# Hybrid decoder layer on one core: products added in pairs in PSUM, the seventh product of a block issued behind the first of the next, three down blocks in seven products, and raw x for the first tile

## The chip, the cores and the metric

The kernel runs on one core of a Trainium2 chip. The metric is the device time of one execution in microseconds (us), as the median of several; lower is better. TensorE (PE) does the matrix products, VectorE (DVE), ScalarE (ACT) and GpSimd (POOL) read and write SBUF, and DVE and ACT also read PSUM, where matrix products end. SyncE (SP) issues most transfers.

## What is computed

```python
def decoder_layer(x, ...):
    h, new_hist, v = hybrid_mixer(rms_norm(x, mix_pre_g), conv_hist, ...)
    x = x + rms_norm(h, mix_post_g)
    f = swiglu(rms_norm(x, ffn_pre_g), w_gate, w_up, w_down)
    return x + rms_norm(f, ffn_post_g), new_hist, v

def hybrid_mixer(xn, ...):
    z = xn @ w_in                                   # 1024 -> 7 x 1024
    u, v, b_gate, c_gate, x_in, r_a, r_b = jnp.split(z, SPLITS, axis=-1)
    u = gelu(u)
    v = layer_norm(gelu(v), sgu_ln_g, sgu_ln_b)
    y_a = (u * chunk_spatial_mix(v, w_s, b_s)) @ w_a_out
    c_in = c_gate * x_in
    y_b = (b_gate * short_conv([conv_hist, c_in], conv_w)) @ w_b_out
    return (sigmoid(r_a) * y_a + sigmoid(r_b) * y_b) @ w_o, ..., v

def swiglu(x, w_gate, w_up, w_down):                # 1024 -> 2816 -> 1024
    return (silu(x @ w_gate) * (x @ w_up)) @ w_down
```

There are 1024 prompt tokens and 8 samples of one token each, all in float32. `rms_norm` multiplies a row by its gain and by the root of its inverse mean square, so the root can also be multiplied in behind a product with a weight.

## The kernel before

**Numbers.** A float32 operand is kept as a high and a low part (`hi`, `lo`, type fp32r), and a product of two operands is three matmuls: hi by hi, hi by lo, lo by hi (`three`).

**Blocks and runs.** Activations lie transposed, channels on partitions, tokens along the free side (two groups of 516, each in two halves of 258 columns with the samples). The weights come in blocks of 256 columns: `B_U` 0, `B_C` 4 (here C, X and B blocks take turns), `B_RA` 16, `B_RB` 20, `B_A` 24 (w_a_out), `B_B` 28 (w_b_out), `B_F` 32 (gate and up blocks in turn), `B_D` 54 to 65 (w_down in three slices of K of `MP` = 4 blocks each, whose sums are added in `g`). `RUNS` lists them; the last blocks are run in two halves (`R_LAST`, `R_LAST + 1`, with 258 columns in their operations). v and w_o are computed in another form, with 512 columns, at the start and in the middle.

**Seven products.** Most blocks are done as Strassen-Winograd, seven products P0 to P6 in place of eight, each of `kps(b)` x 6 matmuls of 258 columns (24 at kps 4, and 18 in the first slice of K, where kps is 3). The operands of the token side are sums and differences of quarters, kept in eight slots of `tp`. The weight side is prepared per run: DVE adds the quarters (`sums`, into `ring_f`), ACT makes the high parts (`prepare`, L1240), POOL the low parts (`ring_lo`, L1095), and PE waits for POOL by `w_lo`. Blocks in `QORDER` are plain: four halves of 48 x kps / 4 matmuls.

**PSUM.** There are four pairs of banks, X, Y, Z and W. `PBANK` says in which pair each product ends. ACT copies P0 (`s1`, L1251), DVE forms from there and from the pairs the four quarters of the result: `c11`, `u1`, `u3`, `u2`, `c22`, `c12`, `c21`, seven operations a run. A product into a pair waits until the pair was read.

**The engines' queues.** Each engine works through one list written out by hand. ACT's has, beside `s1` and `prepare`, the activation functions of the quarters, and where a new stage begins the high parts of its operands: `a_split`, `bt_split`, and `t_split` (L1583) for the three slices of w_down, the wheels here called wheel 0, 1 and 2. DVE's has the low parts `a_rest`, `t_rest` (L2385), and for w_down the additions into `g` (L2484). The operands of the down wheels are written to DRAM as hidden rows are ready and read back by DMA into `tp_f`.

**Start.** The tiles of v are taken in the order samples, then the eight tiles of 128 tokens. Rows are normalised (`x_norm`), turned by PE, split, and multiplied with `wv_hi_t` and `wv_lo_t`, the parts of w_v, whose eight rows of 128 channels come one by one.

## Time and profile before

| | |
|---|---|
| median of 3 runs | 1603.2 us (1603.16 to 1603.54) |
| span of the profiled execution, first to last instruction | 1601.0 us |
| time of a run outside the span (1603.2 - 1601.0) | 2.2 us |
| PE busy | 1590.6 us, 99% |
| DVE, ACT, POOL busy | 1081.9, 559.8, 703.9 us |
| granted TensorE clock, mean | 0.999 of full speed |
| PE's share of the chain that ended last | 95% |

The profile gives for each engine how long it was busy, why it waited and for whom. Since PE is busy for almost the whole span, what counts is the number of matmuls, the time of one, and every moment in which PE waits for a semaphore of another engine. L12 is line 12 of the kernel before.

### The profile page before, as it was taken

The numbers are of one execution on the slowest core, as the hardware profiler recorded it, in microseconds if no ns is written. First come the engines' busy times: TensorE is split into PE (matmuls) and PEld (weight loads), VectorE is DVE, ScalarE is ACT, GpSimd is POOL, SyncE is SP. The second block draws the span as 40 slices with busy tenths as digits, with TensorE's granted clock in tenths as the row PEclk, the third lists the DMA queues.
The fourth block names the chain that finished last, engine by engine and source line by source line (L and its number), as shares of the span: only waits on it lengthen the run. The fifth ranks groups of instructions, "written<-read, shape, count | busy, mean of one in ns | idle before, by whom it ended". The sixth has DMA issues, their size and how long they took to land.

```text
span 1601.0 us, 30253 instructions
## 1 busy us (share of the span) xinstructions
PE 1590.6 (99%) x12427; PEld 1542.2 (96%) x12427; DVE 1081.9 (68%) x1463; ACT 559.8 (35%) x852; POOL 703.9 (44%) x512
## 2 busy tenths in 40 slices
PE   9999999999999999999999999999999999999998
PEld 6889999999999999999978999999999999999997
DVE  8757857797793338868965666766666666575766
ACT  4222332222223336333434532333332233352544
POOL 1011534544544444644730324544444443545375
PEclk9999999999999999999999999999999999999999
DMA  6202011431423333474423313533333345472723
GB/s 216 79 1 80 27 54 34 126 96 44 126 82 110 109 106 121 149 242 133 148 91 120 131 41 110 155 105 100 106 104 104 105 124 178 153 239 80 238 107 133
DMA packets 155283, 184.38 MB, mean 115 GB/s; under 512 B 7355, under 2 KB 138035, under 8 KB 155147
## 3 DMA queue, kind: packets, MB, share of 16 engines
q1 hardware_dynamic: 154987, 182.41, 35.7%
q8 instruction: 99, 1.62, 0.4%
q14 instruction: 37, 0.30, 0.1%
q10 hardware_dynamic: 160, 0.04, 0.0%
HBM read 133.74 MB, written 48.72 MB: 114 GB/s over the span
## 4 chain that ended last, share of the span: by engine, by line
PE 95%; DVE 1%; DMA 1%; POOL 1%; issue 1%; SPq 0%; ACT 0%; DVEq 0%; ACTq 0%; POOLq 0%
PE ps L414 91%; PE ps L449 1%; PE ps L526 1%; DMA pre_gain<-in_mix_pre_g 1%; DVE tp L2213 1%; PE ps L669 0%; PE ps L653 0%; PE ps L424 0%; DMA tp_f<-hid_dram 0%; SPq L783 0%; DVE s_bc L2232 0%; POOL ring_lo L1108 0%; POOL ring_lo L1095 0%; PE ps L503 0%; DVE g L2234 0%
## 5 line engine op out<-in xcount | busy, mean ns | idle before, releaser
L414 PE MATMUL ps<-tp,ring_hi 128*128 128x258 f32 x7292 | 1182.9, 283 | 0.5 <-issue 0.3
L414 PEld LDWEIGHTS ps<-tp,ring_hi 128*128 128x128 f32 x7292 | 1010.6, 190 | 0.9 <-issue 0.5
L414 PE MATMUL ps<-tp,ring_lo 128*128 128x258 f32 x3646 | 744.8, 283 | 0.0
L414 PEld LDWEIGHTS ps<-tp,ring_lo 128*128 128x128 f32 x3646 | 571.3, 190 | 0.0
L1095 POOL TENSOR_TENSOR ring_lo<-ring_f,ring_hi 128x512 fp32r<-128x512 f32 (+1 forms) x228 | 328.3, 1460 | 365.1 <-DVE ring_f L1840 212.5
L1095 POOL TENSOR_TENSOR ring_lo<-stage,ring_hi 128x512 fp32r<-128x512 f32 (+1 forms) x199 | 304.7, 1540 | 400.3 <-ACT ring_hi L1240 399.6
L1240 ACT ACTIVATE ring_hi<-ring_f 128x512 fp32r<-128x512 f32 (+1 forms) x228 | 142.6, 627 | 519.9 <-DVE ring_f L1835 196.2
L1240 ACT ACTIVATE ring_hi<-stage 128x512 fp32r<-128x512 f32 (+1 forms) x199 | 122.0, 617 | 121.1 <-PE ps L414 63.5
L1832 DVE TENSOR_TENSOR ring_f<-stage 128x512 f32<-128x512 f32 (+1 forms) x57 | 46.8, 821 | 135.2 <-PE ps L414 82.7
L1853 DVE TENSOR_TENSOR s_a<-ps,s_a 128x516 f32<-128x516 f32 (+1 forms) x58 | 39.8, 686 | 51.9 <-PE ps L414 51.4
L414 PE MATMUL ps<-tp 128*128 128x512 f32 (+1 forms) x384 | 72.0, 340 | 0.0
L414 PEld LDWEIGHTS ps<-tp 128*128 128x128 f32 x384 | 59.0, 189 | 8.2
L2385 DVE TENSOR_TENSOR tp<-tp_f,tp 128x2064 fp32r<-128x2064 f32 (+1 forms) x24 | 56.2, 2343 | 13.7 <-ACT tp L1583 13.7
L1251 ACT ACTIVATE s_a<-ps 128x516 f32<-128x516 f32 (+1 forms) x58 | 34.2, 590 | 77.3 <-PE ps L414 60.2
L1864 DVE TENSOR_TENSOR s_a<-ps,s_a 128x516 f32<-128x516 f32 (+1 forms) x58 | 39.6, 683 | 30.5 <-PE ps L414 30.4
L1583 ACT ACTIVATE tp<-tp_f 128x2064 fp32r<-128x2064 f32 (+1 forms) x24 | 42.8, 1784 | 39.8 <-DMA tp_f<-hid_dram 33.2
L414 PE MATMUL ps<-wv_hi_t,tp 128*128 128x512 f32 x192 | 54.1, 397 | 0.0
L2420 DVE TENSOR_TENSOR hq<-hq,q 128x516 f32<-128x516 f32 x40 | 47.0, 1176 | 1.1
L1835 DVE TENSOR_TENSOR ring_f<-ring_f,stage 128x512 f32<-128x512 f32 (+1 forms) x57 | 42.8, 751 | 2.2 <-PE ps L414 2.2
L414 PEld LDWEIGHTS ps<-wv_hi_t,tp 128*128 128x128 f32 x192 | 35.7, 188 | 8.0
L1837 DVE TENSOR_TENSOR ring_f<-stage 128x512 f32<-128x512 f32 (+1 forms) x57 | 39.6, 695 | 0.0
L1847 DVE TENSOR_TENSOR s_bc<-ps,s_a 128x516 f32<-128x516 f32 (+1 forms) x21 | 14.0, 668 | 36.8 <-PE ps L414 36.6
(243 smaller groups left out, 1453.9 us busy)
## 6 DMA issues: line engine op xcount, KB each, us to landing
stage<-in_w_in SPq DMA_DIRECT2D x24, 1024.0 KB, 5.9
ht_dram<-ht SPq DMA_DIRECT2D x44, 258.0 KB, 4.2
hid_dram<-hq SPq DMA_DIRECT2D x40, 258.0 KB, 3.1
stage<-in_w_gate SPq DMA_DIRECT2D x10, 1024.0 KB, 6.6
stage<-in_w_up SPq DMA_DIRECT2D x10, 1024.0 KB, 5.3
tp_f<-hid_dram SPq DMA_DIRECT2D x16, 516.0 KB, 5.5
tp_f<-ht_dram SPq DMA_DIRECT2D x16, 516.0 KB, 8.7
stage<-in_w_down SPq DMA_DIRECT2D x8, 1024.0 KB, 7.1
```

Source lines behind the costliest of these rows:

```text
L414: ins = pe.matmul(o, w, xc, start=first and n == 0, stop=last and n == 2)
L1095: pool.tensor_tensor(lo, src, hi.bitcast(f32), SUB).then_inc(w_lo, 1)
L1240: act.activation(w_ring(b, p, kp)[0], src, ACT.Copy).then_inc(w_hi, 1)
L1251: act.activation(s_a[:, gs], reg(Z, gs), ACT.Copy).then_inc(s1_done, 1)
L1583: act.activation(slot(s, 0, both, ks), slot_f(s, 1, both, ks), ACT.Copy).then_inc(t_hi, 1)
L1832: ins = dve.tensor_tensor(out, a21, a22, ADD)
L1835: ins = dve.tensor_tensor(out, ring(ring_f, b, 1, kp), a11, SUB)
L1837: ins = dve.tensor_tensor(out, a11, a21, SUB)
L1853: dve.tensor_tensor(s_a[:, gs], reg(X, gs), s_a[:, gs], ADD).then_inc(u1_done, 1)
L1864: dve.tensor_tensor(s_a[:, gs], reg(Z, gs), s_a[:, gs], ADD).then_inc(u2_done, 1)
L2385: dve.tensor_tensor(slot(s, 1, both, ks), slot_f(s, 1, both, ks), slot_v(s, 0, both, ks), SUB).then_inc(t_lo, 1)
L2420: dve.tensor_tensor(hq[:, n], hq[:, n], q[:, n], MUL).then_inc(hid_ready, 1)
```

## The change

Four parts, in the words of the code:

1. **Wheel.** The first block of each slice of w_down (`B_D`, `B_D + 4`, `B_D + 8`) leaves `QORDER` and runs in seven products. Seven operands a slice stand in place of eight, in slots that turn from slice to slice (`SLOTS_D`), so that product p finds its operand in a slot that an earlier product of the run before has left.
2. **Pairs in PSUM.** P2 is accumulated onto P0 in Y, and P6 onto P4 in X. c11 is then Y as it stands, read by the user itself; `c11` and `u1` are gone as operations of DVE. P2 must wait until ACT has copied P0 (`s1_done`), P6 until `c22` has read P4.
3. **Seventh product behind.** For runs without plain neighbours, P0 of run r + 1 is issued ahead of P6 of run r (`piped`).
4. **v's start.** The samples and the first tile of 128 tokens are multiplied with x times gain, without the root, which comes in as the scale of the gelu. The samples' high and low parts stand in one operand of 40 rows, so that their three matmuls a step become two. The 43 warming transposes of `ident` become 16.

```diff
-PBANK = [Z, W, Y, X, Z, Y, X]
+PBANK = [Y, W, Y, Z, X, Z, X]
...
+D_WHEEL = [5] + SLOTS_B
+SLOTS_D = [[D_WHEEL[(p - n) % 8] for p in range(7)] for n in range(3)]
...
-QORDER.update({b: FIRST_HALF_EVEN for b in (B_D, B_D + MP, B_D + 2 * MP)})
...
+def piped(run):
+    return 2 < run < len(RUNS) - 1 and RUNS[run][0] not in QORDER and RUNS[run + 1][0] not in QORDER
...
+V_STEPS = "S0 H0 s0 S1 H1 L0 s1 S2 H2 L1 s2 S3 H3 L2 S4 H4 s3 L3 N0 S5 H5 s4 S6 H6 s6 s5 H7 s7 S7 " \
+          "L4 L5 L6 N1 L7 l0 l1 l2 l3 l4 l5 N2 l6 l7".split()
...
+            def turn_raw():
+                pe.wait_ge(x_in[0], 16)
+                pe.wait_ge(gain_in, 16)
+                for k in range(KT):
+                    pe.transpose(ps[:, 6, NS * k:NS * k + NS], x_rows[0][0:NS, 128 * k:128 * k + 128], ident[0:NS, 0:NS])
...
             pe.wait_ge(consts, 4)
-            turn_ident(32)
-            turn_norm(0)
-            turn_ident(11)
-            v_sample_tile()
-            v_first_tile(1)
+            turn_ident(8)
+            turn_raw()
+            v_start()
             v_first_tile(2)
...
+            def product(r, p):
+                if p == 6 and piped(r):
+                    issue(r + 1, 0)
+                if p or not piped(r - 1):
+                    issue(r, p)
+
+            def issue(r, p):
...
+                if p == 2:
+                    pe.wait_ge(s1_done, SIDX[r])
+                elif p == 5:
+                    pe.wait_ge(u2_done, SIDX[r])
+                elif p == 6:
+                    pe.wait_ge(c22_done, SIDX[r])
+                elif RUNS[r - 1][0] != b:
+                    bank_free(r - 1, PBANK[p])
...
+            def t_begin(n, r, nb):
+                s1(r)
+                prepare(nb, 0, 2)
+                if n == 1:
+                    c11_down(r)
+                t_split(n, 1)
+                prepare(nb, 2, 3)
+                t_split(n, 2)
...
+                dve.wait_ge(u4_done, SIDX[r])
+                dve.tensor_tensor(c_22, c_22, s_c[:, gs], ADD).then_inc(d_part, 1)
+                dve.tensor_tensor(c_12, c_12, s_c[:, gs], ADD).then_inc(d_part, 1)
+                dve.tensor_tensor(c_21, c_21, s_turn[r % 2][:, gs], ADD).then_inc(d_part, 1)
+                dve.wait_ge(prod_done, done(r, 4))
+                dve.wait_ge(d_part, parts + 1)
+                dve.tensor_tensor(c_22, reg(X, gs), c_22, ADD).then_inc(c22_done, 1)
```

PE's list in the FFN, from P4 of one run to P4 of the next: each row is the first matmul of a product, and in brackets what it waits for. Before:

```order
L414 MATMUL ps<-tp,ring_hi 128x258 [waits s1_done,w_lo]
...
L414 MATMUL ps<-tp,ring_hi 128x258 [waits c11_done,w_lo]
...
L414 MATMUL ps<-tp,ring_hi 128x258 [waits u1_done,w_lo]
...
L414 MATMUL ps<-tp,ring_hi 128x258 [waits u2_done,w_lo]
...
L414 MATMUL ps<-tp,ring_hi 128x258 [waits c22_done,w_lo]
...
L414 MATMUL ps<-tp,ring_hi 128x258 [waits c12_done,w_lo]
...
L414 MATMUL ps<-tp,ring_hi 128x258 [waits c21_done,w_lo]
...
L414 MATMUL ps<-tp,ring_hi 128x258 [waits s1_done,w_lo]
```

In the changed kernel, from P2 of an up block's run (r) to P2 of the next run; the fifth row is P0 of run r + 1, which waits until c11 of run r was read (`hid_ready`), the sixth P6 of run r:

```order
L442 MATMUL ps<-tp,ring_hi 128x258 [waits s1_done,w_lo]
...
L442 MATMUL ps<-tp,ring_hi 128x258 [waits c12_done,w_lo]
...
L442 MATMUL ps<-tp,ring_hi 128x258 [waits c21_done,w_lo]
...
L442 MATMUL ps<-tp,ring_hi 128x258 [waits u2_done,w_lo]
...
L442 MATMUL ps<-tp,ring_hi 128x258 [waits hid_ready,w_lo]
...
L442 MATMUL ps<-tp,ring_hi 128x258 [waits c22_done,w_lo]
...
L442 MATMUL ps<-tp,ring_hi 128x258 [waits u4_done,w_lo]
...
L442 MATMUL ps<-tp,ring_hi 128x258 [waits s1_done,w_lo]
```

The wait for `s1_done` moved from P4 to P2, so that only P6 of the run before and P1 stand between the product that is copied and the one that waits for the copy; P6 waited for `u1_done` and now waits for `c22_done`.

ACT's list where the second slice of w_down begins (wheel 1), around the copy of P0 of the old slice's last block (L1251) and the operands of the new slice (L1583). Before:

```order
L1583 ACTIVATE tp<-tp_f_55 128x8x258 [waits t_in1]
L1251 ACTIVATE s_a<-ps 128x516 [waits c21_done,prod_done]
L1583 ACTIVATE tp<-tp_f_54 128x8x258 [waits t_in0]
L1240 ACTIVATE ring_hi<-stage_71 128x512 [waits prod_done,stage_in0]
L1583 ACTIVATE tp<-tp_f_56 128x8x258 [waits t_in2]
L1240 ACTIVATE ring_hi<-stage_71 128x512 [waits prod_done,stage_in0]
L1583 ACTIVATE tp<-tp_f_50 128x8x258 [waits total_in0]
```

Changed (L1361 is `s1`, L1722 `t_split`, L1414 the new copy of c11, L1331 `prepare`):

```order
L1722 ACTIVATE tp<-tp_f_53 128x8x258 [waits t_in0]
L1361 ACTIVATE s_bc<-ps 128x516 [waits c21_done,prod_done]
...
L1414 ACTIVATE g<-ps 128x516 [waits prod_done]
L1722 ACTIVATE tp<-tp_f_55 128x8x258 [waits total_in0]
L1331 ACTIVATE ring_hi<-stage_71 128x512 [waits prod_done,stage_in0]
L1722 ACTIVATE tp<-tp_f_54 128x8x258 [waits t_in2]
...
L1722 ACTIVATE tp<-tp_f_56 128x8x258 [waits total_in2]
L1331 ACTIVATE ring_hi<-stage_71 128x512 [waits prod_done,stage_in0]
L1361 ACTIVATE s_a<-ps 128x516 [waits c21_done,prod_done]
```

The first operand still stands ahead of `s1` of the last block of the old slice, but P2 of that block waits for this `s1` now, and four operands stand ahead of the copy of P0 of the new slice's first block (the last row), which had no such copy.

DVE's list in a run of the second slice, from the first operation behind c11 to the start of c12. Before (L1853 is u1, L1858 u3, L1864 u2, L1869 c22, L2484 the addition of c22 into `g`, L1835 and L1837 are sums of weights):

```order
L1853 TENSOR_TENSOR s_a<-ps,s_a 128x516 [waits c11_done,prod_done]
L1858 TENSOR_TENSOR s_bc<-ps,s_a 128x516 [waits u1_done]
L1835 TENSOR_TENSOR ring_f<-ring_f,stage_72 128x512 [waits s_sum,stage_in1,prod_done]
L1864 TENSOR_TENSOR s_a<-ps,s_a 128x516 [waits u3_done,prod_done]
L1869 TENSOR_TENSOR s_bc<-ps,s_a 128x516 [waits u2_done,d_tmp]
L1837 TENSOR_TENSOR ring_f<-stage_72 128x512 [waits stage_in1,prod_done]
L2484 TENSOR_TENSOR g<-g,s_bc 128x516 [waits c22_done]
L1875 TENSOR_TENSOR s_bc<-ps,s_bc 128x516 [waits prod_done,u3_done]
```

Changed (L2031 is u2, L2036 u4, L2644 to L2646 the additions of parts, L2649 the new c22):

```order
L2031 TENSOR_TENSOR s_bc<-ps,s_bc 128x516 [waits s1_done,prod_done]
L2036 TENSOR_TENSOR s_bc<-ps,s_bc 128x516 [waits u2_done]
L2019 TENSOR_TENSOR ring_f<-ring_f,stage_71 128x512 [waits s_sum,stage_in0,prod_done]
L2644 TENSOR_TENSOR g<-g,s_bc 128x516 [waits u4_done]
L2645 TENSOR_TENSOR g<-g,s_bc 128x516
L2646 TENSOR_TENSOR g<-g,s_bc 128x516
L2649 TENSOR_TENSOR g<-ps,g 128x516 [waits d_part,prod_done]
L2021 TENSOR_TENSOR ring_f<-stage_71 128x512 [waits stage_in0,prod_done]
```

u1 is gone, and three additions of parts into `g` moved ahead of c22, for which P6 waits.

## Rows read from the trace of the kernel before

**Rows 1.** the page: engines, matmuls of L414 with mean ns of one

```profile
PE 1590.6 (99%) x12427; PEld 1542.2 (96%) x12427; DVE 1081.9 (68%) x1463; ACT 559.8 (35%) x852; POOL 703.9 (44%) x512
...
L414 PE MATMUL ps<-tp,ring_hi 128*128 128x258 f32 x7292 | 1182.9, 283 | 0.5 <-issue 0.3
```

**Rows 2.** PE's waits over the whole span: waited for, us in total, times, longest

```profile
PE ps L509 <- POOL ident L1073: 1.8, 1, 1.8
...
PE ps L414 <- POOL ring_lo L1108: 0.3, 1, 0.3
PE ps L414 <- issue: 0.3, 1, 0.3
PE ps L414 <- POOL ring_lo L1095: 0.3, 1, 0.3
```

**Rows 3.** windows: length, busy us and count for each engine, PEclk, DMA share, GB/s

```profile
200.00:220.24 20.24, 20.24 (x171) 20.24 (x170) 10.90 (x23) 6.04 (x10) 6.47 (x6) 1.00 0.17 53
1410.00:1430.00 20.00, 19.45 (x160) 19.07 (x159) 16.21 (x12) 12.41 (x11) 15.03 (x6) 1.00 1.09 350
```

**Rows 4.** chain that ended last, a piece of the start: start, us, what

```profile
29.67 11.12 PE ps L449 x48
```

**Rows 5.** timeline of PE at the start: start us, us, engine line op

```profile
9.35 0.69 PE L449 MATMUL ps<-wv_hi_t,smp_hi 128*8 128x512 f32 x2
...
34.16 0.62 PE L449 MATMUL ps<-wv_hi_t,tp 128*128 128x512 f32 x2
```

**Rows 6.** timeline of ACT at the start, first row of w_v

```profile
5.31 1.06 ACT L1214 ACTIVATE wv_hi_t<-gv 128x1024 fp32r<-128x1024 f32 x1 [1.39 <-DMA gv<-in_w_in]
```

**Rows 7.** windows of the first 9.35 us, two of them, columns as above

```profile
1.76:4.00 2.24, 2.24 (x11) 2.24 (x12) 0.06 (x1) 1.68 (x4) 0.00 (x0) 1.00 0.73 159
...
7.50:9.35 1.85, 1.85 (x22) 1.75 (x20) 1.08 (x3) 1.51 (x4) 0.25 (x2) 1.00 1.04 425
```

**Rows 8.** timeline of DVE in an FFN pair: c21 of a run

```profile
1129.18 0.69 DVE L1880 TENSOR_TENSOR q<-ps,s_a 128x516 f32<-128x516 f32 x1 [1.53 <-PE ps L414]
```

**Rows 9.** timeline of ACT in the same pair: the silu behind c21

```profile
1129.91 0.64 ACT L1575 ACTIVATE q<-q 128x516 f32<-128x516 f32 x1
```

**Rows 10.** timeline of ACT at the last gate block and the first of w_a_out

```profile
607.69 0.63 ACT L1240 ACTIVATE ring_hi<-stage 128x512 fp32r<-128x512 f32 x1 [0.40 <-PE ps L414]
...
610.90 0.58 ACT L1251 ACTIVATE s_a<-ps 128x516 f32<-128x516 f32 x1
```

**Rows 11.** timeline of DVE at the same place

```profile
620.81 3.45 DVE L2100 TENSOR_TENSOR tp_f<-gv,tp_f 128x1024 f32<-128x1024 f32 x2
624.18 1.26 DVE L2102 TENSOR_TENSOR tp_f<-mix_s,tp_f 128x16 f32<-128x16 f32 x1
```

**Rows 12.** timeline of ACT at the second w_b_out block

```profile
741.57 0.58 ACT L1251 ACTIVATE s_a<-ps 128x516 f32<-128x516 f32 x1
```

**Rows 13.** timeline of DVE at wheel 0

```profile
1359.32 1.76 DVE L2385 TENSOR_TENSOR tp<-tp_f,tp 128x1548 fp32r<-128x1548 f32 x1
```

**Rows 14.** timeline of ACT at wheel 1

```profile
1399.57 0.53 ACT L1240 ACTIVATE ring_hi<-stage 128x384 fp32r<-128x384 f32 x1 [0.43 <-PE ps L414]
1400.00 1.92 ACT L1583 ACTIVATE tp<-tp_f 128x2064 fp32r<-128x2064 f32 x1
1401.82 0.57 ACT L1251 ACTIVATE s_a<-ps 128x516 f32<-128x516 f32 x1
```

**Rows 15.** timeline of DVE at wheel 2

```profile
1496.42 3.10 DVE L2385 TENSOR_TENSOR tp<-tp_f,tp 128x2064 fp32r<-128x2064 f32 x1
1499.44 1.79 DVE L2484 TENSOR_TENSOR g<-g,s_bc 128x516 f32<-128x516 f32 x1
```

**Rows 16.** timeline of DVE at the tail: c21 of R_LAST

```profile
1573.30 0.43 DVE L1880 TENSOR_TENSOR s_bc<-ps,s_a 128x258 f32<-128x258 f32 x1 [0.51 <-PE ps L414]
```

**Rows 17.** timeline of ACT at the tail: table load, last s1

```profile
1575.43 1.28 ACT L1692 ACT_TABLE_LOAD   x1
...
1576.83 0.37 ACT L1251 ACTIVATE s_a<-ps 128x258 f32<-128x258 f32 x1
```

More of the change, by code:

```diff
@@ L409, in _, with three @@
         def _(pe):
-            def three(outs, w_h, w_l, x_h, x_l, first, last):
+            def three(outs, w_h, w_l, x_h, x_l, first, last, onto=False):
                 ins = None
@@ L413, in three @@
                     for o, xc in zip(outs, x):
-                        ins = pe.matmul(o, w, xc, start=first and n == 0, stop=last and n == 2)
+                        ins = pe.matmul(o, w, xc, start=first and n == 0, stop=last and n == 2, skip_group_check=onto)
                 return ins
```

795 lines of the change are left out of this document (450 added, 345 removed).

## The prediction

> **What bounds the kernel now.** I read the page first: PE is busy for 99% of the span, while DVE has 68%, ACT 35% and POOL 44% [rows 1]. The reader should see that the kernel is bound by the number of matmuls and by nothing else on average. The waits of PE come second: one of 1.8 us at the very start, which the change leaves as it is, and three of 0.3 us [rows 2]. So a stall inside can be taken away for less than 1 us, and anything more must come from fewer matmuls. The windows give the time of one: in a steady stretch 168 matmuls (one run of seven products, 24 each) take 20.24 us, 0.1205 us each (the count there has a few over, since a matmul's own duration overlaps the next) [rows 3]. A product is 2.89 us at kps 4, 2.17 us at kps 3, and 1.45 us in the two half runs. A matmul lasts 283 ns by its own row [rows 1], so the end of a product is seen 0.16 us after the next may start. With 512 columns 48 matmuls take 11.12 us, 0.232 us each [rows 4].
>
> **What the change removes.**
> - Down blocks. A plain block has 48 x kps matmuls, one of seven products 42 x kps. Three blocks with kps 3, 4 and 4 lose 6 x 11 = 66 matmuls: 66 x 0.1205 = **-7.95 us**.
> - Start. PE multiplies from 9.35 and reaches the second tile's low-high products at 34.16 [rows 5]. In the changed list the samples need 32 matmuls of 512 columns in place of 48. The first weight row has its high part from 5.31 us on [rows 6]; raw x of the first tile is turned by about 6.6, multiplied by the gain by 7.9 and split by 9.0, by ACT and DVE operations as long as those of the list before (1.06 us at ACT). The samples' first matmul can start at about 7.75, and from there 80 matmuls (samples 32, first tile 48) x 0.232 = 18.6 us and three turns of about 0.9 us are worked off with about 0.9 us of waits: 29.95. That is **-4.2 us** against 34.16. Bounds: -4.5 if nothing waits, -2.5 if the clock takes part (below).
> - The stalls at 812 and 1417 to 1421: the places are relieved (seven operands a slice, two DVE operations fewer a run). **-0.85 us** [rows 2], bounds 0 and -0.9.
>
> Together -13.0 us.
>
> **What it adds: shorter leashes.** PE must now find three things ready in each run: the copy of P0 (`s1`) before P2, u2 before P5, c22 before P6. I laid the lists of the changed kernel over the durations of the trace.
> - Steady runs, no stall. Let T be the end of P6. c21 takes 0.69 [rows 8], the silu behind it 0.64 [rows 9], `s1` 0.58 [rows 10]: done at T + 2.0. P2 starts at T + 2.73 (P1's 2.89 less 0.16). That leaves 0.7 us, and a prepared block (0.63 at ACT) fits in but no more. Some 50 runs look like this. Cost 0; if the cover were gone it would be paid 50 times, so it is the first thing to look at afterwards.
> - From the r_b blocks to w_a_out. P6 of the run before the last ends at 610.5 (607.6, where ACT's next weight row waits for PE [rows 10], plus the P0 put before it). c21, a gate and `a_split` of about 2.1 us stand ahead of `s1`, which ran from 610.90 to 611.5 before; it ends at 614.4 now where P2 could start at 613.2: 1.2 us. Then P6 and the plain halves of w_a_out, which follow at once, wait for c22 and c12, and these stand behind `a_rest` and the totals, 3.45 + 1.26 us where POOL works too [rows 11]. I get 1.9 us at least and 5.2 at most in sum, and take **+3.0**, above the lower end because the trace shows DVE's list full there.
> - w_b_out. `s1` of its second block ran from 741.57 to 742.15 behind an operand [rows 12], and P2 would start at about 741.0; P6 of the run before w_b_out waits 0.25 us. **+1.2** (0.4 to 2.2).
> - Wheel 0. u2 of the last FFN run stands behind `t_rest` (1.76 us each at kps 3 [rows 13]) and the totals of the hidden rows. **+1.0** (0 to 3).
> - Wheel 1. An operand of 1.92 us stands between a weight row and `s1`: the three ran from 1399.57 to 1402.39 [rows 14], T + 2.9, and P2 starts at T + 2.0, since P1 is of kps 3 here: +0.9. The next `s1` stands behind four operands and the last weight row, whose sum is made behind c12: +0.8 (0 to 2). **+1.7**. The operands land fast enough, with the DMA at 350 GB/s [rows 3].
> - Wheel 2. The same with kps 4: +0.36 for the first; the second `s1` waits for a sum behind c12, three additions into `g` (0.69 to 1.79 each) and two `t_rest` of 2.9 and 3.1 us [rows 15]: +1.5 (0.5 to 3.2). **+1.9**.
> - Tail. In `R_LAST` the copy stands behind c21, a square and a gain, T + 2.35 where P2 could start at T + 1.29 (P1 is 1.45 long): +1.05. In `R_LAST + 1` a table load stands there too: from c21 at 1573.30 [rows 16] to the end of `s1` at 1577.20 [rows 17] it took 3.9 us, of which 0.75 (the addition now made by c21 itself) goes, 3.15 against 1.29: +1.85. P6 behind the root of y: +0.3 (0 to 0.7). **+3.2**, bounds 2.0 and 3.7.
>
> DVE's u2 and c22 in steady runs come 2 us ahead of their need (T + 9.4 against T + 11.6), because two operations of 0.69 are gone.
>
> **The sum.** -13.0 + 3.0 + 1.2 + 1.0 + 1.7 + 1.9 + 3.2 = -13.0 + 12.0 = **-1.0 us**. Against the profiled execution: 1601.0 to 1600.0. The median is 2.2 us above that span, and nothing in the change touches what lies around it: 1603.2 - 1.0 = **1602.2 us**. At the lower bounds of the stalls (1.9, 0.4, 0, 0.9, 0.86, 2.0: 6.1) it is 1596.3; at the upper bounds (5.2, 2.2, 3, 2.9, 3.6, 3.7: 20.6) 1610.8.
>
> **A rule that speaks against the change.** DVE's additions of two inputs in SBUF take 1.79 us instead of 0.69, and a 16-column one 1.26 us, where GpSimd works at the same time [rows 15, 11]. The Trainium skill, "SBUF — State Buffer", section "Who interferes with whom", calls the port pair of DVE and GpSimd an exclusive lock that is held for a whole instruction, and the trace agrees as far as that 16-column operation waits about 1.1 us, no more than a GpSimd operation lasts. By that rule the three additions of parts that moved ahead of c22 could wait for GpSimd up to three times, 1.1 us each; that would be the upper bound at wheels 1 and 2, and is a way into the slower rival.
>
> **The rivals.**
> - *Stalls at their lower bounds.* DVE loses two operations of 0.69 us a run; its lists at the wheels may be so much earlier that only ACT's order costs. For it speaks that PE shows almost no stall now, though the lists are as full. Against it: at the tail and at wheel 1 the lateness is ACT's own, and 2.9 us are left whatever DVE does. Time about 1596.5 (1594 to 1599).
> - *Slower: ACT's queue at wheels 1 and 2.* `s1` of the new slice's first block stands behind a weight row whose sum DVE makes behind c12. c12 can't come before P5, and if DVE's additions run at 1.8 us in place of 0.69, three of them and two `t_rest` delay the sum by about 4 us. Each microsecond in which the sum ends later than 0.85 us before P6's end is a microsecond for PE. That is 3 us more at each of two wheels: 1602.2 + 6 = 1608. For it: the 1.79 and 3.10 us rows. Against it: the seven operands arrive over a whole run, and the additions may fall between GpSimd's.
> - *The clock at the start.* The windows say that the granted clock was 1.00 from the first, which is 2.4 GHz, yet 11 transposes took 2.24 us (0.20 each) in the first window, and 22 took 1.85 us (0.084 each) just before the samples [rows 7]. PE had then worked without a pause. With 16 warming transposes in place of 43, and waits for x between them, the first matmuls of v may still go at the slow pace: at about double the time, 7 or 8 pairs lose some 0.23 us a matmul, up to 3 us. The time would be about 1605. The Trainium skill, "TensorE: Matmul & The Clock Gate", Part 1, says that throttled is the default and activity releases it; the pace of the transposes agrees and the row of the granted clock doesn't. I count it 1 in 10, because PE is busy for some 5 of the 6 us before.
> - *The change doesn't save its matmuls* is excluded: the order of PE's list holds 66 and 16 fewer.
>
> **How the numbers follow.** 0.2% is 3.2 us, about what a measurement of this kernel can tell from no change. The forecast (stalls eat nearly all, 1598.5 to 1606) gets 0.47, of which 0.12 lie under 1600, 0.32 within and 0.03 above; the first rival 0.28, nearly all faster; the slower one 0.15; the clock 0.10, half within and half above. Together faster 0.38, same 0.39, slower 0.23. The range 1595.5 to 1609 leaves out the last of either side.
>
> **What would show it.** Right: the second tile's matmuls near 30 us; PE stalls of 1 to 3 us at about 610 to 630, 740, wheels 1 and 2 and in the last 30 us, released by ACT's `s1` or DVE's c22; none in the FFN. Wrong: PE waits in every FFN run (then 50 times any of it), `s1` never named among PE's releasers (then the time is that of the first rival), or matmuls at half pace before 12 us. Accumulating onto a bank that ACT has just read is shown by no row here. The 258-column matmuls of one product already accumulate without a gap, so I take 0 for it; a cost of only 0.2 us a run, some 50 times, would put the time above my range.

## The result and the profile after

The changed kernel took 1625.7 us (median of 4 runs, 1624.9 to 1627.5), the kernel before 1603.4 (4 runs, 1603.2 to 1603.6): a ratio of 1.0139, 95% interval 1.0125 to 1.0154. It is slower by 22.4 us. Forecast were 1602.2 us and a range of 1595.5 to 1609, with a chance of 0.23 for slower, so the prediction was wrong, and outside its range. The profiled execution has a span of 1624.6 us; L12 is now line 12 of the changed kernel.

The page, engines and the product's own matmuls (answers to [rows 1]):

```profile
PE 1589.9 (98%) x12335; PEld 1540.6 (95%) x12335; DVE 1001.5 (62%) x1376; ACT 558.1 (34%) x867; POOL 722.7 (44%) x524
...
L442 PE MATMUL ps<-tp,ring_hi 128*128 128x258 f32 x7248 | 1182.3, 285 | 23.1 <-ACT s_bc L1361 5.2
```

PE is as busy as before (1590.6 us there) with 92 records of matmuls fewer (66 are saved in the down blocks and 16 in the samples; the rest are transposes at the start), and the line of the products has 23.1 us of idle time ahead of it where it had 0.5. So two things happened: PE waits, and a part of its matmuls lasts longer. PE's waits (answers to [rows 2], without the two at the very start and end that both kernels have) say for whom:

```profile
PE ps L442 <- ACT s_bc L1361: 5.2, 5, 1.5
PE ps L442 <- DVE g L2649: 4.7, 3, 2.2
PE ps L442 <- ACT s_a L1361: 4.2, 3, 1.8
PE ps L442 <- DVE s_a L2042: 3.5, 1, 3.5
PE ps L442 <- DVE s_a L2031: 3.3, 1, 3.3
PE ps L442 <- DVE q L2042: 2.2, 1, 2.2
PE ps L488 <- ACT raw_hi L1366: 1.9, 1, 1.9
...
PE ps L442 <- POOL ring_lo L1199: 0.2, 1, 0.2
```

The changed code waits in 14 places inside (all the L442 rows with ACT or DVE as releaser), in sum 23.1 us. ACT's copy of P0 (L1361, `s1`) has 9.4 us of it, DVE's c22 (L2042, in the wheels L2649) 10.4, u2 (L2031) 3.3. None of them lies in the FFN between 1000 and 1300 us. The windows (columns as in [rows 3]) show where matmuls last longer:

```profile
10.43:14.40 3.97, 3.97 (x10) 2.33 (x11) 3.90 (x6) 3.97 (x6) 1.10 (x1) 0.57 1.03 412
200.00:220.24 20.24, 20.24 (x171) 20.24 (x170) 10.15 (x23) 6.89 (x12) 5.88 (x6) 1.00 0.16 53
627.00:633.00 6.00, 5.38 (x32) 5.41 (x33) 4.16 (x7) 3.14 (x4) 0.61 (x1) 0.72 0.00 0
1374.00:1384.00 10.00, 6.74 (x36) 6.57 (x35) 8.83 (x11) 3.00 (x6) 3.42 (x4) 0.66 0.50 160
1540.00:1544.00 4.00, 3.74 (x19) 3.77 (x20) 1.92 (x4) 3.25 (x6) 1.94 (x2) 0.57 0.02 4
```

In a steady stretch the product is what it was: 20.24 us with 171 records, like the first of [rows 3]. Around four places the granted clock is lowered, and around 717 us as well (0.59 from 716.7 to 720.8); the mean over the span (0.993) hides it. Inside each stretch it is 0.50 for 3.4 us, that is 1.2 GHz, and PE had stood idle just before: 1.94 us at the start, 2.25, 3.50, 3.26 and 2.21 us inside. Wheel 0 has two such stretches in a row, so inside there are five. A 258-column matmul takes 0.215 us there instead of 0.1205 (E5 shows the rows), so 16 are done in 3.4 us, which would take 1.9: a stretch costs 1.5 us where PE is busy through all of it. Wheel 0's two lasted from 1376.24 to 1383.07 by the record of the clock, and PE stood idle until 1377.46, so together they cost 2.5; the one in wheel 2, from 1540.08, cost 1.4. The five inside cost 6.9 us.

**The account.** Fixed points of the program say where the time came from: the transposes of `hist_rows` come at 105.41 us (106.6 before, -1.2), the first product of w_o comes at 806.88 (795.5, +11.4), eight products of `ones` and `q` in the tail at 1601.91 (1578.84, +23.1). A stall costs 0.24 us more than the idle time that the view shows, here called its trail: 0.16 because a matmul's shown end trails the next possible start, and 0.08 because the second matmul behind a stall starts late as well (0.195 us after the first, in E5 too). By terms: matmuls saved -7.95, start -1.2, 14 stalls +23.1, their trails +3.4, five stretches +6.9, the stalls of before with their trails -1.6, one new wait for `ring_lo` +0.5: +23.1 against +23.6 between the spans. 0.5 us is open.

What lies behind the stalls is seen in the engines' lists. DVE at the first w_a_out blocks (answers to [rows 11]; L2254 is `a_rest`, L2042 c22):

```profile
617.69 2.35 DVE L2254 TENSOR_TENSOR tp<-gv,tp 128x1024 fp32r<-128x1024 f32 x2
619.97 0.17 DVE L2256 TENSOR_TENSOR tp<-mix_s,tp 128x16 fp32r<-128x16 f32 x1
...
622.26 3.46 DVE L2254 TENSOR_TENSOR tp<-gv,tp 128x1024 fp32r<-128x1024 f32 x2 [0.79 <-ACT tp L1475]
625.64 1.23 DVE L2256 TENSOR_TENSOR tp<-mix_s,tp 128x16 fp32r<-128x16 f32 x1
626.79 0.68 DVE L2042 TENSOR_TENSOR q<-ps,q 128x516 f32<-128x516 f32 x1
```

PE has been idle since 625.4, ready for P6. c22 comes at 626.79 because `a_rest` stands ahead of it, and its last two rows take 3.46 and 1.23 us where the same two took 2.35 and 0.17 just before; GpSimd's next low parts run from 622.82 to 626.84.

At w_b_out the delay begins in SP's queue (L973 loads of gate rows, L956 the first operands of w_b_out):

```profile
685.77 16.04 SPq L973 DMA_DIRECT2D q<-ra_dram  x4
...
702.88 5.88 SPq L956 DMA_DIRECT2D tp_f<-ob_dram  x3
```

The loads of `ob_dram` were issued at 702.88, behind four gate loads whose issues stretch over 16.04 us from 685.77; before, they were issued at 696.50. That is 6.4 us later, of which 4.0 is what the whole program had lost by then; the rest goes with the gate loads, the last of which may start only when the last quarter of a run is gated, and this quarter comes from P6, behind P0 (2.89 us) of the next run. In E4, where P6 stands in its own place, `ob_dram` is issued at 696.32, and PE is as far on there as in the kernel before. ACT's `b_split` starts at 711.74 (704.23 before), and on DVE its low part stands ahead of c22:

```profile
713.70 2.31 DVE L2317 TENSOR_TENSOR tp<-tp_f,tp 128x2064 fp32r<-128x2064 f32 x1 [4.76 <-ACT tp L1529]
715.93 0.69 DVE L2042 TENSOR_TENSOR s_a<-ps,s_bc 128x516 f32<-128x516 f32 x1
```

DVE in wheel 1, up to c22 (L2649; L2545 is `t_rest`, L2644 to L2646 the additions of parts; answers to [rows 15]):

```profile
1448.05 3.41 DVE L2545 TENSOR_TENSOR tp<-tp_f,tp 128x2064 fp32r<-128x2064 f32 x1
1451.38 1.77 DVE L2644 TENSOR_TENSOR g<-g,s_bc 128x516 f32<-128x516 f32 x1
1453.08 0.68 DVE L2645 TENSOR_TENSOR g<-g,s_bc 128x516 f32<-128x516 f32 x1
...
1454.29 0.68 DVE L2649 TENSOR_TENSOR g<-ps,g 128x516 f32<-128x516 f32 x1
```

The operation on the operand and the first addition are drawn out (3.41 and 1.77 us) while GpSimd works, until 1452.60; the next takes 0.68. What this drawing out alone costs PE no run shows, since none moves GpSimd's work there. PE waits 2.18 us, until 1455.12. In wheel 0 two `t_rest`, a sum of weights and totals of the hidden rows stand ahead of u2, the last of them the first row here:

```profile
1374.94 1.76 DVE L2545 TENSOR_TENSOR tp<-tp_f,tp 128x1548 fp32r<-128x1548 f32 x1
1376.63 0.69 DVE L2031 TENSOR_TENSOR s_a<-ps,s_a 128x516 f32<-128x516 f32 x1
```

At the start PE took the slow turns up to 7.77 and then waited (answers to [rows 5, 7]):

```profile
6.48 1.53 PE L528 MATMUL ps<-ident,x_rows 128*128 128x128 f32 x8
...
10.43 0.85 PE L488 MATMUL ps<-wv_hi_t,raw_hi 128*128 128x512 f32 x2 [1.94 <-ACT raw_hi L1366]
...
32.86 0.97 PE L477 MATMUL ps<-wv_hi_t,tp 128*128 128x512 f32 x3 [0.19 <-ACT tp L1312]
```

### The profile page after: what moved, and what is told of

The parts are those of the page before. It is cut to its first block, busy times and chain, and to the rows that moved or that the text cites. A ratio compares the mean times of both kernels' runs of the same rounds, so it can differ in the third digit from the quotient of the medians.

```text
span 1624.6 us, 30012 instructions
## 1 busy us (share of the span) xinstructions
PE 1589.9 (98%) x12335; PEld 1540.6 (95%) x12335; DVE 1001.5 (62%) x1376; ACT 558.1 (34%) x867; POOL 722.7 (44%) x524
## 4 chain that ended last, share of the span: by engine, by line
PE 88%; DVE 6%; issue 2%; ACT 2%; DMA 1%; POOL 0%; DVEq 0%; SPq 0%; ACTq 0%; POOLq 0%
PE ps L442 83%; DVE tp L2545 2%; PE ps L488 1%; PE ps L587 1%; PE ps L477 1%; DMA tp_f<-ob_dram 1%; PE ps L454 0%; PE ps L759 0%; ACT tp L1722 0%; PE ps L743 0%; DVE tp L2375 0%; DVE g L2644 0%; DVE ring_f L2019 0%; ACT tp L1474 0%; PE ps L572 0%
## 5 line engine op out<-in xcount | busy, mean ns | idle before, releaser
L442 PE MATMUL ps<-tp,ring_hi 128*128 128x258 f32 x7248 | 1182.3, 285 | 23.1 <-ACT s_bc L1361 5.2
L442 PEld LDWEIGHTS ps<-tp,ring_hi 128*128 128x128 f32 x7248 | 1009.7, 191 | 25.8 <-issue 17.3
L442 PE MATMUL ps<-tp,ring_lo 128*128 128x258 f32 x3624 | 743.0, 284 | 0.0
L442 PEld LDWEIGHTS ps<-tp,ring_lo 128*128 128x128 f32 x3624 | 570.5, 191 | 0.0
L1186 POOL TENSOR_TENSOR ring_lo<-ring_f,ring_hi 128x512 fp32r<-128x512 f32 (+1 forms) x240 | 348.9, 1475 | 356.1 <-DVE ring_f L2024 209.7
L1186 POOL TENSOR_TENSOR ring_lo<-stage,ring_hi 128x512 fp32r<-128x512 f32 (+1 forms) x196 | 293.0, 1504 | 415.7 <-ACT ring_hi L1331 415.1
L1331 ACT ACTIVATE ring_hi<-ring_f 128x512 fp32r<-128x512 f32 (+1 forms) x240 | 150.0, 625 | 535.7 <-DVE ring_f L2019 182.2
L1331 ACT ACTIVATE ring_hi<-stage 128x512 fp32r<-128x512 f32 (+1 forms) x196 | 120.7, 619 | 253.6 <-PE ps L442 185.3
L2016 DVE TENSOR_TENSOR ring_f<-stage 128x512 f32<-128x512 f32 (+1 forms) x60 | 58.2, 970 | 104.1 <-DMA stage<-in_w_in 53.9
L442 PE MATMUL ps<-tp 128*128 128x512 f32 (+1 forms) x384 | 72.1, 340 | 0.0
L442 PEld LDWEIGHTS ps<-tp 128*128 128x128 f32 x384 | 59.0, 189 | 8.2
L2053 DVE TENSOR_TENSOR q<-ps,s_a 128x516 f32<-128x516 f32 x17 | 11.8, 696 | 72.2 <-PE ps L442 72.2
L442 PE MATMUL ps<-wv_hi_t,tp 128*128 128x512 f32 x192 | 54.1, 397 | 0.0
L2021 DVE TENSOR_TENSOR ring_f<-stage 128x512 f32<-128x512 f32 (+1 forms) x60 | 51.8, 864 | 0.0
L2545 DVE TENSOR_TENSOR tp<-tp_f,tp 128x2064 fp32r<-128x2064 f32 (+1 forms) x21 | 51.1, 2435 | 0.0
L2031 DVE TENSOR_TENSOR s_bc<-ps,s_bc 128x516 f32<-128x516 f32 (+1 forms) x31 | 21.2, 685 | 47.0 <-PE ps L442 47.0
L2031 DVE TENSOR_TENSOR s_a<-ps,s_a 128x516 f32<-128x516 f32 (+1 forms) x30 | 20.5, 685 | 42.5 <-PE ps L442 42.3
L442 PEld LDWEIGHTS ps<-wv_hi_t,tp 128*128 128x128 f32 x192 | 35.6, 188 | 8.0
L2024 DVE TENSOR_TENSOR ring_f<-stage,ring_f 128x512 f32<-128x512 f32 (+1 forms) x60 | 40.3, 671 | 0.0
L1722 ACT ACTIVATE tp<-tp_f 128x2064 fp32r<-128x2064 f32 (+1 forms) x21 | 37.4, 1781 | 5.5 <-DMA tp_f<-hid_dram 3.7
L1186 POOL TENSOR_TENSOR tp<-tp_f,tp 128x512 fp32r<-128x512 f32 x4 | 5.7, 1464 | 61.5 <-ACT tp L1331 61.5
```

Of the source, the lines that this page charges most:

```text
L442: ins = pe.matmul(o, w, xc, start=first and n == 0, stop=last and n == 2, skip_group_check=onto)
L1186: pool.tensor_tensor(lo, src, hi.bitcast(f32), SUB).then_inc(w_lo, 1)
L1331: act.activation(w_ring(b, p, kp)[0], src, ACT.Copy).then_inc(w_hi, 1)
L1722: act.activation(slot(s, 0, both, ks), slot_f(s, 1, both, ks), ACT.Copy).then_inc(t_hi, 1)
L2016: ins = dve.tensor_tensor(out, a21, a22, ADD)
L2021: ins = dve.tensor_tensor(out, a11, a21, SUB)
```

## The experiments

Each ran beside the kernel before on the same chip; ratios are to that kernel. E1 to E4 ran together, E5 to E8, E9 and E10.

### E1: `s1` put ahead of the operands

```diff
-                if last:
-                    a_split(1)
                 s1(r)
                 if last:
+                    a_split(1)
                     a_split(0)
...
             prepare(B_B + 1, 4, 6)
+            s1(B_B + 1)
             bt_split(3)
             prepare(B_B + 1, 6)
-            s1(B_B + 1)
...
+                s1(r + 1)
                 t_split(n, 4)
                 prepare(nb, 6)
...
-            for e in range(12, 16):
+            for e in range(12, 15):
                 sq_gain(e)
-            act.activation(warm, eps, ACT.Sqrt)
             s1(R_LAST + 1)
+            sq_gain(15)
+            act.activation(warm, eps, ACT.Sqrt)
```

> The changed kernel with ScalarE's copy of P0 (s1) put ahead of what stands before it in ACT's list at the six places where PE waited for it: ahead of a_split(1), bt_split(3), t_split(1,0), t_split(1,4), t_split(2,0), t_split(2,4), and at the tail ahead of the last square and gain and of the table load. Theory A (s1 is late because of what is queued before it on ACT, 9.4 us of stalls in all, and nothing else is late at these places): these seven waits go, 1625.7 - 9.4 = about 1616.5. Rival B (the runs behind them are late for DVE as well, so that the stall moves to the next c22): under half is given back, 1621 or more. The stalls on c22 and u2 (about 10.4 and 3.3 us) and four of the five stretches at the halved clock stay.

Measured: 1623.1 us (1620.7 to 1624.0), 1.0117 [1.0102, 1.0132]. PE's waits in it:

```profile
PE ps L442 <- DVE g L2652: 6.9, 4, 3.2
PE ps L442 <- DVE s_a L2034: 4.1, 3, 3.3
PE ps L442 <- DVE q L2045: 3.6, 1, 3.6
PE ps L442 <- DVE s_a L2045: 3.2, 1, 3.2
...
PE ps L442 <- ACT s_bc L1361: 0.2, 1, 0.2
```

ACT's copies had 9.4 us and have 0.2. The waits for c22 and u2 had 13.7 us and have 18.1, and seven stretches at half clock stand inside where there were five (+2.6 us). So 9.2 us and their trails taken away shortened the span by 2.8: half only moved to the next wait, which was late on its own account, and the longer waits cost more clock. That is rival B. The copy alone is not the cause of the loss.

### E2: c22 put ahead of the operands

```diff
+                c22(r, q[:, 3], q[:, 1])
                 if last:
                     a_rest(2)
-                c22(r, q[:, 3], q[:, 1])
...
+                if last:
+                    b_rest(1)
...
                 dve.tensor_tensor(c_22, reg(X, gs), c_22, ADD).then_inc(c22_done, 1)
+                sums(nb, 1)
+                if n is not None:
+                    t_rest(n, 1)
...
+                dve.tensor_tensor(c_12, c_12, s_c[:, gs], ADD).then_inc(d_part, 1)
+                dve.tensor_tensor(c_21, c_21, s_turn[r % 2][:, gs], ADD).then_inc(d_part, 1)
...
+                    t_rest(0, 5)
+                    u2(r + 2)
                 hidden_total(j, 2, hq)
                 hidden_total(j, 1, hq)
```

> The changed kernel with DVE's list reordered: c22 ahead of a_rest(2), ahead of b_rest(1), and in the down runs ahead of a weight sum and of two of the three additions into g; at wheel 0 t_rest(0,5) and u2 ahead of the last three hidden totals. Theory A (DVE's own order makes P6 and P5 wait, and each such stall of over 2 us also costs 1.7 us at the halved clock): 2.2 + 3.5 + 2.2 + 2.2 of c22 go, the 3.3 of u2 falls to about 1, and with them about 8 us of halved clock: 1625.7 - 12.4 - 8 = about 1605. Rival B (the clock's loss has nothing to do with these stalls): 1613. Rival C (DVE is simply full there, so that the wait moves on to the next read): over 1616.

Measured: 1624.7 us (1624.2 to 1626.0), 1.0130 [1.0115, 1.0145].

```profile
PE ps L442 <- ACT s_bc L1361: 9.0, 6, 2.8
PE ps L442 <- ACT s_a L1361: 5.2, 3, 1.9
PE ps L442 <- DVE s_bc L2048: 2.9, 1, 2.9
PE ps L442 <- DVE q L2048: 2.3, 1, 2.3
```

c22 is gone from the waits at both boundaries and in the last two wheels, wheel 0's stall for u2 fell from 3.3 to 0.8 us, and still the waits inside sum to 23.1 us again: 2.9 and 2.3 for c12 (L2048) at the boundaries, where the plain halves of w_a_out and w_b_out need its bank first, 14.2 for ACT's copies in place of 9.4, one of them 2.8, 1.6 for c22 at 1380.9 in the first slice, where it was not waited for before, and 1.1 at 480 us for a weight block that landed late. Three stretches at half clock stand inside, where there were five. Neither list alone carries the loss; behind the delay in one stands one of the same size in the other. The time is that of rival C, the wait moved on, though not to DVE's reads alone.

### E3: work for PE in the gap of the start

```diff
                         if k == 7:
                             ins.then_inc(v_full, 1)
+                        if n == 0:
+                            turn_ident(16)
```

> The changed kernel with 16 transposes of ident put between the first matmuls of the samples and the first of the raw tile, where PE was idle for 1.9 us before a stretch at half clock. Theory A (the halved clock behind the idle stretch is what makes the start late): the wait remains, the halved stretch goes, 1.7 us less: 1624.0. Rival B (the clock falls whatever PE does there, or the transposes run slowly and push the first matmul back): same or up to 1 us slower.

Measured: 1625.8 us (1624.3 to 1628.2), 1.0137 [1.0122, 1.0153].

```profile
10.43:14.40 3.97, 3.97 (x24) 2.67 (x22) 3.94 (x6) 3.97 (x5) 0.72 (x1) 1.00 1.02 414
```

```profile
23.34 0.64 PE L488 MATMUL ps<-wv_lo_t,smp_v 128*8 128x512 f32 x2 [0.65 <-POOL wv_lo_t L1167]
...
32.83 2.36 PE L477 MATMUL ps<-wv_hi_t,tp 128*128 128x512 f32 x9 [0.19 <-ACT tp L1314]
```

With transposes in the gap the clock stays at 1.00 (0.57 in the changed kernel). That alone doesn't show that the idle time lowered it: in E1, E2, E4 and E7 the start is as in the changed kernel, PE is idle there for 1.55 to 1.67 us, and the clock stays at 1.00 too. What it cost is shown by all five: the second tile comes at 32.80 to 32.83 us, as behind the lowered clock (32.86), and PE waits 0.65 to 0.97 us at 23.3 us for GpSimd's low parts of w_v, of which it makes two in 9.6 us. The time didn't move. At the start the lowered clock lay within the wait for GpSimd, and cost nothing.

### E4: P6 back in its own place

```diff
-    return 2 < run < len(RUNS) - 1 and RUNS[run][0] not in QORDER and RUNS[run + 1][0] not in QORDER
+    return False
```

> The changed kernel with the seventh product in its old place: P6 of a run is issued before P0 of the next. All else stays. Theory A (piping is what makes the copy of P0 late, since P6 ends one product later, c21 and what ACT makes of it come later, and only P1 stands between): the seven waits for s1, 9.4 us, go, while P6 has one product less of cover for c22: 4 of the c22 stalls grow by up to 2.9 us each, less what SP's queue gains in front of w_b_out: between 1616 and 1628, and the FFN stays without stalls. Rival B (the piping is what covers c22 in every run): a stall in each of some 50 runs, 0.5 us or more each, 1650 or more.

Measured: 1625.6 us (1624.5 to 1627.4), 1.0133 [1.0116, 1.0150]. In PE's waits c22 in the wheels has this row:

```profile
PE ps L442 <- DVE g L2649: 11.6, 7, 3.8
```

Of ACT's copies only two are waited for, 1.5 and 0.4 us, since two products, P0 and P1, stand between P6 of the run before and P2, and not one. c22 is waited for 16.5 us with its other rows, where it was 10.4, since P6 comes a product earlier, and seven stretches at half clock stand inside. Taken out alone, the third part of the change is neither gain nor loss here, to within about 4 us.

### E5: a ladder of stalls in the kernel before

To price a stall and find from which length the clock falls, additions into a scratch row of DVE stand ahead of u1 in seven FFN runs of the kernel before, 7 to 13 of them. Their results aren't used.

```diff
+                for _ in range({3: 7, 4: 8, 5: 9, 6: 10, 7: 11, 8: 12, 9: 13}.get(j, 0)):
+                    link(dve.tensor_tensor(s_c[:, :], s_a[:, :], s_a[:, :], ADD))
                 u1(r)
```

> The kernel before, with DVE's u1 made late in seven FFN gate runs, 40 us apart, by 7, 8, 9, 10, 11, 12 and 13 extra additions of 128x516 (some 0.75 us each) ahead of it; their result is not used. PE then has stalls that differ by about 0.75 us from rung to rung, from about 0.5 to about 5 us, in a stage that has none. Theory A (a stall has two prices, its own length, and above some length between 1.5 and 2.3 us a further 1.7 us in which the matmuls go at the halved clock): the rungs above it show a stretch with a granted clock of 0.5 behind the stall and lose 1.7 us, those above about 3 us lose up to 3.4; those below show none. Rival B (the halved clock in the changed kernel has another cause): no stretch at a lower clock on any rung.

Measured: one run of 1620.5 us, span 1618.8, 17.8 longer than the span before. It has no second execution, so its price per stall rests on this one trace. The two shortest gave no stall, the others 0.44, 1.17, 1.89, 2.63 and 3.36 us (ending at 1126.9, 1168.9, 1211.5, 1256.3 and 1301.8). The windows behind three of them:

```profile
1168.00:1173.00 5.00, 4.16 (x34) 4.19 (x35) 4.93 (x8) 1.58 (x3) 1.29 (x1) 1.00 0.00 0
1211.00:1216.00 5.00, 4.52 (x25) 4.55 (x26) 4.77 (x8) 1.91 (x4) 1.30 (x2) 0.66 0.01 3
1301.00:1308.00 7.00, 6.16 (x31) 6.20 (x31) 6.04 (x9) 3.27 (x6) 2.66 (x3) 0.54 0.00 1
```

The stall of 1.17 us left the clock at 1.00; those of 1.89 and 2.63 us (1256 to 1260: 0.57) went with one stretch at 0.50, the one of 3.36 with two, the first of which began 1.2 us before PE went on. Behind the third, on PE's timeline:

```profile
1212.57 1.06 PE L414 MATMUL ps<-tp,ring_hi 128*128 128x258 f32 x4
...
1213.86 1.06 PE L414 MATMUL ps<-tp,ring_hi 128*128 128x258 f32 x4
```

Six matmuls stand between the starts of two groups, in 1.29 us: 0.215 each. By the starts of its matmuls PE lost 0.68, 1.40, 3.57, 4.31 and 6.05 us at the five: the stalls sum to 9.5 us, their trails to 5 x 0.24 = 1.2, and the four stretches to 5.3. With a longer wait for `ring_lo` (1.5) and 0.2 at the start that is 17.7 of the 17.8. So a stall costs 0.24 us more than its length where the clock holds, 1.7 more with one stretch and 2.7 with two. The Trainium skill, "TensorE: Matmul & The Clock Gate", Part 1, says that the throttled clock is the default and activity releases it; the ladder agrees, in that the lower level came back only with idle time of PE. A length from which it falls can't be read from it: in the changed kernel 2.18 and 1.81 us (at 1455.1 and 1598.9) brought no stretch, and in E9 not even 2.98 and 3.33 us, while in E7 1.94 and 1.81 us did.

### E6: the start's low part moved from GpSimd to DVE

```diff
-WV_POOL = (3, 5)
-WV_DVE = (0, 1, 2, 4, 6, 7)
+WV_POOL = (3,)
+WV_DVE = (0, 1, 2, 4, 5, 6, 7)
...
-                turn_ident(8)
+                turn_ident(4)
...
+            wv_rest(5)
```

> The changed kernel with the low part of the sixth row of w_v made by DVE and not by GpSimd, and with 4 warming transposes in place of 8 ahead of the raw tile's own. In the three experiments before, GpSimd's two low parts took 9.6 us together and PE waited for the second, whether or not the clock had fallen before; the second tile began at 32.8 us every time. Theory A (GpSimd's low part sets the end of the start): the second tile begins near 31.3, and the time is 1.0 to 1.5 us less, 1624.5. Rival B (DVE gets it done later, since it already has the roots to make): same.

Measured: 1624.9 us (1621.9 to 1627.1), 1.0131 [1.0113, 1.0150]. The second tile on PE:

```profile
31.21 3.99 PE L477 MATMUL ps<-wv_hi_t,tp 128*128 128x512 f32 x16 [0.36 <-ACT tp L1312]
```

It comes 1.65 us earlier, with a gap of 1.48 us behind which the clock stays at 1.00. The transposes of `hist_rows` come at 103.72 us, 1.7 earlier than in the changed kernel. The total moved by 0.8 us, less than its own spread. That the start was bound by GpSimd is shown by the trace; that the whole time gains by it is not shown.

### E7: E2 with banks that fit

In E2 the plain halves of w_a_out and w_b_out began with bank pair Z, the one that c12 reads last.

```diff
+AB_BANK = [W, Y, Z, X]
...
-                half(B_A, i, PLAIN_BANK[i], lambda q: (a_lo, (2, 1, 3, 4)[q]))
+                half(B_A, i, AB_BANK[i], lambda q: (a_lo, (2, 1, 3, 4)[q]))
```

> The experiment with c22 first in DVE's list (1624.7), and the plain halves of w_a_out and w_b_out put into the banks in the order W, Y, Z, X in place of Z, W, Y, X. There PE waited 2.3 and 2.9 us for c12 to free Z for the first half, and once at halved clock. Theory A (the order of the banks is stale: with pairs in PSUM, W and Y are free first): both waits and 1.7 us of halved clock go, 6.9 us less, 1617.8. Rival B (DVE is full, and the second or third half waits as long): 1622 or more.

Measured: 1622.3 us (1620.4 to 1623.2), 1.0113 [1.0098, 1.0128].

```profile
PE ps L443 <- ACT s_bc L1362: 9.1, 6, 3.0
...
PE ps L443 <- issue: 1.7, 2, 1.1
```

The waits of 2.9 and 2.3 us for c12 became 1.1 and 0.6, and the next copy of P0 is waited for 3.0 us instead of 1.5, with two stretches at half clock, from 746.14 on. That is within rival B's forecast, 1622 or more. Again the time moved one place on.

### E8: all of it together

E1 (also in the third slice), E2 (also c22 in the first slice's first block, ahead of a sum of weights), E7 and E6 in one kernel. What is new:

```diff
+                    s1(r + 1)
                     prepare(b + 1, 6)
-                    if mp == MP - 2:
-                        s1(R_LAST)
                     sq_gain(e + 3)
...
                 if mp == 0:
                     t_rest(0, 6)
+                    dve.wait_ge(hid_saved[3], 16 * J)
+                    c22(r, g[:, m + 1, 1], g[:, m, 1])
                 sums(b + 1, 1)
```

> All together: the copy of P0 first (in the third slice of w_down ahead of the fourth square in each run), c22 first, the banks W, Y, Z, X, and the start with only one low part on GpSimd. Theory A (lists and bank order alone, not the four parts of the change, make the loss): stalls of the changed kernel of 23 us go down to about 5, with one or two stretches at halved clock (2 to 3 us): 1625.7 - 18 - 6 - 1.5 = about 1600, faster than before (1603.4). Rival B (the work of DVE around the wheels can't be placed in less time): the c22 waits of the down wheels stay at about 3 us each with halved clock, 1609 or more.

Measured: 1605.3 us (10 runs, 1604.4 to 1606.9), 1.0011 [1.0002, 1.0021].

```profile
PE ps L443 <- ACT s_bc L1362: 3.1, 4, 1.4
PE ps L443 <- issue: 2.2, 2, 1.3
```

No stall inside is over 1.44 us, and no stretch inside has a lowered clock. E1, E2, E6 and E7 took 0.8 to 3.4 us off the changed kernel's median, all together take off 20.4. That is the chain of delays from the other side: the waits go only when ACT's list, DVE's list and the banks are all early. The two moves that are new here were not tried alone, nor were E1 and E2 without the others, so the shares of the 20.4 us aren't shown. No run takes the wheels or the pairs in PSUM out alone either; that the lists and banks, and not these parts, made nearly all of the loss is shown by E8, which keeps all four parts.

### E9: E8 with P6 in its own place

The edit is that of E4.

> The experiment with everything together (1605.3), without piping: P6 of a run ahead of P0 of the next. Theory A (once c22 stands early in DVE's list, piping is worth little either way, as it was in the changed kernel, where it moved 9.4 us of waits from c22 to s1 and back): within 3 us of 1605.3. Rival B (with the lists right, piping gives P6 the cover it needs): the c22 stalls of the down wheels come back, with halved clock, 1612 or more.

Measured: 1611.5 us (1609.3 to 1612.1), 1.0045 [1.0031, 1.0058]. c22 is waited for five times, 0.9 to 3.3 us, twice in this row:

```profile
PE ps L443 <- DVE g L2648: 5.6, 2, 3.3
```

Rival B is right on these waits. Of the halved clock one stretch came, at 1438.10, with a stall of 2.25 us. The stall of 3.33 us, which ended at 1524.96, left the clock as it was:

```profile
1524.90:1530.00 5.10, 5.04 (x42) 5.07 (x43) 5.10 (x7) 3.42 (x6) 1.94 (x2) 1.00 0.02 5
```

Once the lists are right, the seventh product behind the next first one is worth 0.34% of the time, about 5.5 us, or 2.8 to 8.1 with the two intervals combined (E8 and E9 ran on different chips, each against the kernel before); by E4 it seemed worth nothing.

### E10: four more moves in ACT's list

```diff
-                    prepare(r + 1, 0, 2)
+                    prepare(r + 1, 0, 3)
                     at_split(1)
-                    prepare(r + 1, 2, 3)
...
+                    prepare(r + 1, 0, 2)
                     b_split(3)
-                    prepare(r + 1, 0, 1)
                     b_split(0)
-                    prepare(r + 1, 1, 2)
                     b_split(2)
...
-            prepare(B_B + 1, 4, 6)
+            prepare(B_B + 1, 4, 5)
             s1(B_B + 1)
+            prepare(B_B + 1, 5, 6)
...
+                    if mp == 0:
+                        s1(r + 1)
                     prepare(b + 1, 5, 6)
                     sq_gain(e + 2)
-                    s1(r + 1)
+                    if mp:
+                        s1(r + 1)
```

> The experiment with everything together, and four more moves in ACT's list: three high parts of w_a_out's weights ahead of at_split(1) and two of w_b_out's ahead of b_split(3), where PE waited 1.3 and 0.9 us at the second half for a low part; the copy of P0 of the second w_b_out block ahead of one more weight row (0.7 us), and that of the second block of the third slice ahead of a weight row and a square (1.4 us). Theory A (these are late by list order alone): 4.3 + 4 x 0.16 less, 1605.3 - 4.5 = about 1600.8, faster than before by 0.15%. Rival B (DVE and GpSimd are full there and each wait moves on by one product): over 1603.5, not faster than before.

Measured: 1602.6 us (11 runs, 1600.9 to 1604.5) against 1603.8 (15 runs): 0.9993 [0.9984, 1.0002], no difference that can be told.

```profile
PE ps L443 <- DVE s_a L2037: 2.2, 3, 1.0
PE ps L443 <- ACT s_bc L1362: 2.1, 3, 1.1
```

Thirteen waits are left inside, 6.8 us in sum, one over 1 us (1.14, a copy of P0 in the second w_a_out block). By terms: matmuls -7.95, start -2.9 (at the transposes of `hist_rows`), waits +6.8 and trails +3.1, the stalls of before -1.6: -2.5, where the spans show -1.5 and the medians -1.2. About 1 us of it stays open, in E8 too. So the remaining waits use up most of what the change can give; a version that beats the kernel before by a measurable amount wasn't found.

## Why the prediction was wrong

**The frame held.** PE's matmuls bound both kernels, the seven-product runs kept their pace, the FFN has no stall, accumulating onto a bank just read costs nothing that shows (2491 matmul records between 1000 and 1300 us in both kernels), and every stall lies at a place that has a term in the sum: 613 to 628, 717, 752, the three wheels, the last 30 us. Removed matmuls -7.95 and the relieved stalls stand. A wait of 1.06 us for `x_late` near the end, which the prediction's list of PE's waits leaves out, is 1.07 us in the changed kernel and plays no part.

**The terms on `s1` were right in the main.** Forecast 1.2 in the r_b to w_a_out boundary, measured 1.14; 0.9 and 0.91 at wheel 1's first; 0.36 and 0.29 at wheel 2's; 1.85 and 1.81 in `R_LAST + 1`. Larger than said were 1.44 in `R_LAST` (1.05), 1.47 in the second w_b_out block (about 0.95) and 1.41 at wheel 1's second (0.8); smaller was 0.99 at wheel 2's second (1.5). In sum 9.5 against 8.6.

**The failed step is P6 behind c22, and P5 behind u2, at the boundaries.** The prediction costed c22 at 0.25 us in w_b_out, at 0.3 in the tail, at about 1.8 with c12 at r_b to w_a_out, and at nothing in wheels 1 and 2, where both terms are on `s1`; u2 had 1.0 in wheel 0. That is 3.4 us, and PE waited 13.7: 2.25 and 3.50 at the two boundaries, 3.26 for u2 in wheel 0, 2.18 and 2.21 in wheels 1 and 2, 0.28 in the tail. For the steady runs it had said that "DVE's u2 and c22 in steady runs come 2 us ahead of their need", and the trace of the changed kernel bears it out (in one FFN run u2 ends at 1112.26, 2 us ahead of P5, and c22 at 1115.14, even 5 us ahead of P6). At the boundaries DVE's list has two to four more operations ahead of c22, and that lead is used up. Step by step, with trails and without the clock: r_b to w_a_out 3.9 (forecast 3.0), w_b_out 5.5 (1.2), wheel 0 3.5 (1.0), wheel 1 5.2 (1.7), wheel 2 4.2 (1.9), tail 4.2 (3.2): 26.5 against 12.0, of which 3.4 are trails, for which the sum has no term. At w_b_out the step missed was the queue of SP: the move of P6 put a gate load late, and the operand's load stood behind it. I had not followed the transfers that wait for the quarter which P6 brings.

**The second failed step is the clock inside, costed at 0.** I had the clock as a rival at the start alone, where E3 shows that it cost nothing. Inside it took 6.9 us. [Rows 2] show no stall of before over 0.3 us inside, so no row of before had the price; E5 gave it: 1.5 us on top of a stall that brings one stretch, 2.5 with two.

**The start gave 1.2 us of the 4.2.** The wait for `raw_hi` was 1.9 us, not 0.9, because the turns before ran slowly (8 in 1.53 us, and 8 of `ident` in 1.97). The sign that the prediction gave for its rival of the clock did come, matmuls at half pace before 12 us (0.50 from 10.91 to 14.32), but not its cost: with the clock at 1.00 (E1 to E4, E7) the second tile came no earlier, since GpSimd's two low parts of w_v, 9.6 us, set it, and in E6, with one of them, it came at 31.21. The prediction hadn't looked at GpSimd there at all. It also misread [rows 7]: the second window holds 8 narrow turns of the samples, so 0.084 us is no pace of a transpose. Between starts of transposes of `ident` the trace has 0.213 us up to 6.27 and 0.109 from there, just half.

**The slower rival** had the right places and rows for wheels 1 and 2 (DVE's additions and operands drawn out to 1.8 and 3.4 us ahead of something that PE waits for), and nearly their price: 6 us more forecast, 5.8 more measured. It hung on ACT's sum, though, where c22 itself was late, and it knew nothing of w_b_out, wheel 0 and the clock, which brought 4.3, 2.5 and 6.9 us beyond the forecast. So the nearness of its price is in part luck, and its 1608 was still 18 us short.

**What E1, E2 and E7 add:** the terms of the sum weren't independent. A stall that is taken away lets PE arrive earlier at the next wait, whose releaser didn't move, so E1's removals gave 2.8 us of 9.2. As an account of one trace such a sum is fair; as a guide to what a repair is worth it failed.
